# Second layer of a two-layer trunk: scores on 64 rows of the array, half of the projections and of the output projection placed between the attention steps

## The reference, cut to what matters

```python
def diff_attend(q, k, v, lam):
    s = jnp.einsum('bqhcd,bkhcd->bchqk', q, k).astype(jnp.float32) * HEAD_DIM ** -0.5
    p = jax.nn.softmax(s, axis=-1)
    a = (p[:, 0] - lam * p[:, 1]).astype(v.dtype)
    return jnp.einsum('bhqk,bkhv->bqhv', a, v)

# diff_attn_layer, the x branch (the layer's ctx output isn't needed)
q, k, v, g = jnp.split(h @ w_in, 4, axis=-1)      # k, v also of ctx
q = apply_rope(rms_norm(q, q_norm), cos, sin); k = apply_rope(rms_norm(k, k_norm), cos, sin)
o = diff_attend(q, k_all, v_all, lam)             # 512 queries, 768 keys
o = rms_norm(o, head_norm) * (1.0 - lambda_init)
x = x + gate * ((o * jax.nn.silu(g)) @ w_out)
```

## Time and profile before

| what | value |
|---|---|
| runs | 1311.74, 1316.6, 1316.97 us (median 1316.6) |
| the profiled execution, its own time | 1307.97 us |
| its span | 1306.1 us |
| busy in the span: PE, PE weight loads | 1234.6 us (95%), 673.1 us (52%) |
| DVE, ACT, POOL | 613.9 us (47%), 347.3 us (27%), 210.9 us (16%) |
| second layer's projections (window 791 to 1011) | PE busy 219.93 of 220 us |
| attention (window 1015 to 1247) | PE busy 219.50 of 232 us |
| output projection (window 1247 to 1302) | PE busy 54.97 of 55 us |

### The profile page before, as it was taken

The page is one execution under the profiler, slowest core; times in us unless marked ns, Lnnn a source line. Parts: engine busy times, 40 slices in busy tenths (PEclk is TensorE's granted clock), DMA queues, the critical chain, the costliest instruction groups (busy, mean ns, idle before and its releaser), DMA issues.

```text
span 1306.1 us, 12218 instructions
## 1 busy us (share of the span) xinstructions
PE 1234.6 (95%) x4455; PEld 673.1 (52%) x4455; DVE 613.9 (47%) x1224; ACT 347.3 (27%) x750; POOL 210.9 (16%) x198
## 2 busy tenths in 40 slices
PE   3699999999999999999899998999999999999988
PEld 0455566655555444555544444444444456667643
DVE  0466661368686645656711125330024444677712
ACT  1311112112221233335600012110011344566600
POOL 2100001567661300000000002230013000000000
PEclk9899999999999999999999999999999999999999
DMA  9601111034444011001000303110111110000001
GB/s 313 255 1 37 65 64 65 1 115 144 162 161 154 1 49 49 1 1 49 1 0 1 113 7 134 65 64 1 65 64 65 64 64 1 1 1 2 33 25 40
DMA packets 40464, 81.48 MB, mean 62 GB/s; under 512 B 2470, under 2 KB 3975, under 8 KB 40407
## 3 DMA queue, kind: packets, MB, share of 16 engines
q1 hardware_dynamic: 36165, 68.83, 15.0%
q10 hardware_dynamic: 3122, 8.57, 1.8%
q0 software_dynamic: 1120, 3.32, 0.9%
HBM read 78.58 MB, written 2.13 MB: 62 GB/s over the span
## 4 chain that ended last, share of the span: by engine, by line
PE 89%; DVE 5%; DMA 3%; ACT 2%; issue 1%; SPq 0%; POOLq 0%; POOL 0%; ACTq 0%; DVEq 0%
PE ps L623 42%; PE ps L859 9%; PE ps L800 6%; PE ps L886 6%; PE ps L906 3%; PE ps L753 3%; PE ps L842 3%; PE ps L782 3%; PE ps L769 2%; PE ps L897 2%; PE ps L662 2%; DMA ring<-in_mod_w_dram 1%; PE ps L823 1%; PE ps L833 1%; PE ps L816 1%
## 5 line engine op out<-in xcount | busy, mean ns | idle before, releaser
L623 PE MATMUL ps<-ring,hT 128*128 128x512 f32 (+1 forms) x960 | 397.2, 574 | 2.7 <-DVE hT L1016 1.3
L623 PEld LDWEIGHTS ps<-ring,hT 128*128 128x128 f32 x960 | 181.7, 190 | 208.7 <-issue 202.0
L623 PE MATMUL ps<-hT,ring 128*128 128x256 f32 (+1 forms) x512 | 169.2, 488 | 3.5 <-DVE pool_mem L1032 2.0
L1610 POOL TENSOR_SCALAR stat<-stat 128x8 f32<-128x8 f32 (+3 forms) x52 | 21.8, 419 | 768.7 <-DVE stat L1178 228.0
L623 PEld LDWEIGHTS ps<-hT,ring 128*128 128x128 f32 x512 | 96.1, 190 | 73.2 <-issue 65.8
L886 PE MATMUL ps<-pool_mem 128*128 128x512 f32 (+1 forms) x256 | 93.0, 487 | 1.3 <-ACT pool_mem L1547 1.3
L800 PE MATMUL ps<-ring,hT 128*128 128x512 f32 x192 | 89.3, 595 | 3.7 <-DVE pool_mem L1246 3.6
L1178 DVE TENSOR_REDUCE stat<-pool_mem 128x8 f32<-128x512 f32 (+1 forms) x26 | 18.6, 714 | 156.3 <-ACT pool_mem L1465 156.3
L859 PE MATMUL ps<-ring,hT 128*128 128x512 f32 x192 | 84.6, 593 | 1.6 <-DMA ring<-in_ev_w_out_dram 1.6
L1282 DVE TENSOR_TENSOR pool_mem<-ps,pool_mem 128x512 f32<-128x512 f32 x20 | 13.8, 691 | 138.0 <-PE ps L859 92.3
L1220 DVE TENSOR_REDUCE stat<-ps 128x1 f32<-128x768 f32 x64 | 61.1, 954 | 24.6 <-PE ps L886 24.4
(11 more groups left out here) (191 smaller groups left out, 1469.0 us busy)
## 6 DMA issues: line engine op xcount, KB each, us to landing
ring<-in_mod_w_dram SPq DMA_DIRECT2D x11, 2048.0 KB, 8.4
ring<-in_od_w_in_dram SPq DMA_DIRECT2D x8, 2048.0 KB, 7.9
ring<-in_ev_w_in_dram SPq DMA_DIRECT2D x7, 2048.0 KB, 7.9
ring<-in_ev_w_out_dram SPq DMA_DIRECT2D x4, 1536.0 KB, 6.7
ring<-in_od_w_out_dram SPq DMA_DIRECT2D x2, 2048.0 KB, 7.8
ring<-in_mod_w_dram ACTq DMA_DIRECT2D x1, 2048.0 KB, 15.6
xs_all<-in_x_dram POOLq DMA_DIRECT2D x4, 512.0 KB, 9.4
xs_all<-in_x_dram ACTq DMA_DIRECT2D x4, 512.0 KB, 5.4
```

The source lines that it names most:

```text
L623: mm = pe.matmul(bank[:, 0:width], lhs_of(k), rhs_of(k), start=(k == 0), stop=(k == count - 1))
```

## The change

The reference isn't changed, nor is the first layer. In the second:

- A score of one component uses only its 64 rows: queries are copied whole into `qT1` (one copy in place of two half copies, no zeroed halves), and the matmul takes rows 0 to 63 or 64 to 127 of both operands. All four score matmuls of a step stand together, alternating between components, and TensorE's stage for component 1 is empty. They wait for both exponentials of the step before.
- There is one probability buffer; transposes and value products belong to step n-1 in place of n-2, and the exponentials of step n wait for the transposes of step n-1. `comb1` is of step n itself.
- Before the attention stand only the first column halves of k1, q1, v1 (heads 0 to 3): 16 units. The rest, with g1, are 24 units between steps 0 and 19 (two in steps 1, 2, 3 and 9, one in the others). Their norm and rotary turn is a stage of its own, `rope`, which stands in the next step between `exp1` and `comb1`. The squares have two buffers.
- In a head's last step, the turns stand behind `exp1` in place of before it.
- `hnorm` and `otr` of a head are handed out in the same step, from step 12 on: heads 0, 1, 2 in steps 12, 13, 14, heads 3 to 6 in steps 16, 20, 24, 28, right behind the head's last `pv1`.
- The output projection is split over heads: `out1a` (heads 0 to 3, four matmuls a unit, 8 units: one in each of steps 21, 22, 24, 25, 27, 28 and two after the last step) and `out1` (heads 4 to 7, 8 units at the end). VectorE adds both to x.
- The gates' transfers and their sum come earlier (steps 11 and 16).

```diff
@@ stages_layer1
-    st += [("k1", n, t) for n in range(2) for t in range(NT)]
-    st += [("v1", n, t) for n in range(2) for t in range(NT)]
-    st += [("q1", n, t) for n in range(2) for t in range(NX)]
-    fill = [("g1", n, t) for n in range(2) for t in range(NX)]
+    for kind, tiles in (("k1", NT), ("q1", NX), ("v1", NT)):
+        for t in range(tiles):
+            st += [(kind, 0, t)] + ([("rope", kind, 0, t)] if kind != "v1" else [])
+
+    fill = [("g1", 0, 0)] + [u for t in range(1, 4) for u in (("g1", 0, t), ("k1", 1, t - 1))]
+    fill += [("k1", 1, t) for t in range(3, NT)]
+    fill += [("q1", 1, t) for t in range(NX)] + [("v1", 1, t) for t in range(NT)]
+    gate_fill = [("g1", 1, t) for t in range(NX)]
+    early_out = [("out1a", n, t) for n in range(2) for t in range(NX)]
...
-    for n in range(len(work) + 2):
+    for n in range(len(work) + 1):
         if n < len(work):
-            st.append(("sc1",) + work[n] + (0,))
-        if n >= 2:
-            st.append(("ptr1",) + work[n - 2])
+            st += [("sc1",) + work[n] + (c,) for c in range(2)]
+        if n >= 1:
+            st.append(("ptr1",) + work[n - 1])
         if n < len(work):
             h, t = work[n]
-            st.append(("sc1", h, t, 1))
+            st.append(("exp1", h, t))
             if t == NX - 1 and h < C_HEADS - 1:
                 st += [("hk", h + 1, 1), ("hq", h + 1), ("hk", h + 1, 0)]
-            st.append(("exp1", h, t))
...
+            st += ropes
+            ropes = []
+            st.append(("comb1", h, t))
+        now = []
+        if n < 16:
+            now = [fill.pop(0) for _ in range(1 + (n in (1, 2, 3, 9)))]
+        elif n < 20:
+            now = [gate_fill.pop(0)]
+        elif early_out and n % 3 != 2:
+            now = [early_out.pop(0)] if len(early_out) > 2 else []
+        st += now
+        ropes += [("rope",) + u for u in now if u[0] in ("k1", "q1")]
+        if n >= 1:
+            st.append(("pv1",) + work[n - 1])
+            if work[n - 1][1] == NX - 1:
+                late += [("hnorm", work[n - 1][0]), ("otr", work[n - 1][0])]
...
+        if n >= 12 and n < len(work):
+            for _ in range(2):
+                if late:
+                    st.append(late.pop(0))
+    st += late[:1] + early_out + late[1:]
     st += [("out1", n, t) for n in range(2) for t in range(NX)]
@@ tensor engine
                 elif kind == "sc1":
...
+                    if c == 1:
+                        continue
                     if n == 0:
                         pe.wait_ge(prob_ready, len(SCORE))
-                    if n >= 2:
-                        pe.wait_ge(prob1_ready, n - 1)
+                    else:
+                        pe.wait_ge(prob1_ready, n)
...
                     for lo, hi in ((0, 512), (512, TOK)):
-                        mm = pe.matmul(pair(n)[:, lo:hi], qpad[:, c, t * P:(t + 1) * P], kT1[:, lo:hi],
-                                       start=True, stop=True)
-                    mm.then_inc(sc_ready, 1)
+                        for comp in range(2):
+                            half = slice(comp * HD, (comp + 1) * HD)
+                            mm = pe.matmul(pair(n + comp)[:, lo:hi], qT1[half, t * P:(t + 1) * P], kT1[half, lo:hi],
+                                           start=True, stop=True)
+                            if hi == TOK:
+                                mm.then_inc(sc_ready, 1)
...
+                    (w,) = slabs(stage)
+                    project(stage, SLAB, lambda k: oT[first + k][:, a[1] * P:(a[1] + 1) * P],
+                            lambda k: w[:, first + k, :], C_HEADS // 2)
@@ scalar engine
-                        A.copy(qpad[0:HD, 0, :], bank[0:HD, :])
-                        A.copy(qpad[HD:P, 1, :], bank[HD:P, :]).then_inc(done_sem(stage), 1)
+                        A.copy(qT1, bank).then_inc(done_sem(stage), 1)
...
-                        if n < 4:
-                            act.wait_ge(qk_ready, len(HEADU))
-                        else:
-                            act.wait_ge(pt1_ready, n // 2 - 1)
-                        A.activation(place[:, c, :], pair(n)[:, 0:TOK], ACT.Exp, bias=nmax[:, r:r + 1],
+                        if n >= 2:
+                            act.wait_ge(pt1_ready, n // 2)
+                        A.activation(prob1[:, c, :], pair(n)[:, 0:TOK], ACT.Exp, bias=nmax[:, r:r + 1],
                                      scale=SCALE, accum_out=rsum[:, r:r + 1]).then_inc(prob1_ready, 1)
```

More of the change, by code:

```diff
@@ L177, in stages_layer1 @@
-        if 1 <= n <= len(work):
-            st.append(("comb1",) + work[n - 1])
-        if fill and (n < 4 or n % 2 == 0):
-            st.append(fill.pop(0))
-        if n >= 2:
-            st.append(("pv1",) + work[n - 2])
-            if late and not fill:
-                st.append(late.pop(0))
-            if work[n - 2][1] == NX - 1:
-                late += [("hnorm", work[n - 2][0]), ("otr", work[n - 2][0])]
-            if work[n - 2] == (C_HEADS - 1, 1):
-                st.append(("gates", 1))
@@ L189, in stages_layer1 @@
-    st += late + [("gatesum", 1)]
+                if h + 1 == 3:
+                    st.append(("gates", 1))
+            st += ropes
[10 more added lines that the diff above has]
+        ropes += [("rope",) + u for u in now if u[0] in ("k1", "q1")]
@@ L215 @@
 UNIT_STAGES = ("params", "mod", "modsum", "modcol", "xbc", "kvdt", "dt", "q", "ga", "z", "pv", "ytr", "out0",
-               "k1", "v1", "q1", "g1", "hq", "hk", "pv1", "otr", "out1")
+               "k1", "v1", "q1", "g1", "hq", "hk", "pv1", "otr", "out1a", "out1")
 UNITS = [s for s in STAGES if s[0] in UNIT_STAGES]
@@ L235, in slabs_of @@
         return [(kind, stage[1])]
+    if kind == "out1a":
+        return [("out1", stage[1])]
     return []
@@ L868, in _ @@
                     pe.wait_ge(qk_ready, NT + HEADN[("q1", h // 4, NX - 1)] + 1)
-                    turn(stage, [q1v[:, t, h * P:(h + 1) * P] for t in range(NX)])
+                    turn(stage, [q1v[:, h // 4, t, h % 4 * P:(h % 4 + 1) * P] for t in range(NX)])
                 elif kind == "hk":
                     h, s = a
-                    pe.wait_ge(qk_ready, NT + HEADN[("k1", 1, NT - 1)] + 1)
-                    turn(stage, [k1v[:, t, h * P:(h + 1) * P] for t in (range(NX) if s == 0 else range(NX, NT))])
+                    pe.wait_ge(qk_ready, NT + HEADN[("k1", h // 4, NT - 1)] + 1)
+                    turn(stage, [k1v[:, h // 4, t, h % 4 * P:(h % 4 + 1) * P]
+                                 for t in (range(NX) if s == 0 else range(NX, NT))])
                 elif kind == "sc1":
@@ L901, in _ @@
                     pe.wait_ge(pt1_done, at(*stage))
-                    if stage == ("pv1", 0, 0):
-                        wait_done_upto(pe, ("v1", 1, NT - 1))
+                    if t == 0 and h % 4 == 0:
+                        for tile in range(NT):
+                            wait_done(pe, ("v1", h // 4, tile))
                     bank = begin(stage)
@@ L911, in _ @@
                     turn(stage, [g1v[:, t, a[0] * P:(a[0] + 1) * P] for t in range(NX)])
-                elif kind == "out1":
+                elif kind in ("out1a", "out1"):
+                    first = 0 if kind == "out1a" else C_HEADS // 2
                     if a == (0, 0):
-                        wait_done_upto(pe, ("otr", C_HEADS - 1))
-                    token_major(stage, a[1])
+                        for h in range(first, first + C_HEADS // 2):
+                            wait_done(pe, ("otr", h))
+                    (w,) = slabs(stage)
+                    project(stage, SLAB, lambda k: oT[first + k][:, a[1] * P:(a[1] + 1) * P],
+                            lambda k: w[:, first + k, :], C_HEADS // 2)
         @block.vector
@@ L1279, in _ @@
                         tmp, gate = res_tmp1[:, u % 2, :], gate_bc1[:, n * SLAB:(n + 1) * SLAB]
+                    if stage == ("out1", 0, 0):
+                        dve.wait_ge(early_ready, 2 * NX)
                     if u >= 2:
-                        dve.wait_ge(x1_ready if kind == "out0" else out_ready, u - 1)
+                        dve.wait_ge(told, u - 1)
                     V.tensor_tensor(tmp, bank_of(stage), gate, ALU.mult).then_inc(done_sem(stage), 1)
@@ L1284, in _ @@
                     part = x1[:, t, n * SLAB:(n + 1) * SLAB]
-                    V.tensor_tensor(part, part, tmp, ALU.add).then_inc(x1_ready if kind == "out0" else out_ready, 1)
+                    V.tensor_tensor(part, part, tmp, ALU.add).then_inc(told, 1)
                 elif kind == "g1":
@@ L1305, in _ @@
                                                 in1=rsum[:, r:r + 1], op0=ALU.mult, op1=ALU.mult))
[L1306 removed]
+                    p0, p1 = (prob1[:, c, :] for c in range(2))
                     V.scalar_tensor_tensor(out=p0, in0=p1, scalar=rinv[:, r + 1:r + 2], in1=p0,
@@ L1555, in _ @@
                     h, t = a
-                    place = prob1[at(*stage) % 2]
```

(2 more changed lines are left out.)

59 lines of the change are left out of this document (31 added, 28 removed).

## The result

| | kernel before | changed kernel |
|---|---|---|
| median (lowest to highest) | 1313.03 us (1307.8 to 1316.97), 10 runs | 1321.05 us (1316.58 to 1326.4), 10 runs |
| ratio | | 1.006, interval 1.0038 to 1.0082 |
| profiled execution: time, span, granted clock | 1307.97, 1306.1, 0.996 | 1319.4, 1316.8, 0.984 |

The change made the kernel slower by 0.6%. I had forecast 5 us less; it is 8 us more. The time lies inside the range, but the sign is wrong.

A forecast was written before the change was run, and what follows sets the result against it. TensorE was taken to bound the second layer; 456 us of work plus 50 of waits gave 506 in place of 511.1, moving the median 5 us to 1311.5. The 8-in-10 range was 1296 to 1327.

The forecast's parts named there:

- the sign: Whole kernel: median to move 5 us down to 1311.5; chances faster 0.36, within 0.5% 0.40, slower 0.24.
- Scores: Second layer's attention: both components run side by side, 1.29 us a step, 41.3 us less work.
- rivals of partial and no pairing: Each step's four score matmuls: partial overlap gives 1325 (chance 0.08), no overlap +41, 1353 (chance 0.07).
- the 1.72 us: Scores of a step if passes start strictly in turn: 1.72 in place of 1.29, 13.8 more in all.
- Change of the array's shape: Going in and out of 64-row scores costs 0.20 us a step, 6.4 in all; bounds 0 and 0.3.
- Waits: TensorE's waits in the second layer, listed by place: 50 us after the change, 20 before.
- step 10's: Two rotary turns after step 9's two q units end comb1 at 13.4; 1.75 us of wait come through.
- late first passes: After each of some 25 waits the first pass runs late by about 0.08 us: 2 us.
- granted clock 1.00 throughout: Listed among the signs that would show the forecast right: the granted clock stays at 1.00.
- the clock as a rival: Steps from 20 on: clock drop over half of 95 us costs about 25 us, giving 1336; chance 0.04.
- the 506 forecast: Second layer, start to start: 456 us of work plus 50 of waits, in place of 511.1.
- longer waits: Rival: each of the eleven long waits is longer by 1 us, giving 1322; chance 0.05.

The follow-up runs named there:

- e6: Changed kernel with both components' scores computed on rows 0 to 63, so nothing can run side by side: 1376.31 us, ratio 1.048 to the kernel before.
- e4: Changed kernel with matmuls whose result nobody reads inside TensorE's waits before third turns and otr: 1308.64 us, ratio 0.9964 to the kernel before.
- e9: Kernel before, unedited, profiled a second time: 1314.24 us, ratio 1.0008.
- e1: Changed kernel with only the turns put back in front of the exponentials: 1303.12 us, ratio 0.9926 to the kernel before.
- e2: Changed kernel with only otr moved one step behind its hnorm: 1299.13 us, ratio 0.9895 to the kernel before.
- e3: Changed kernel with turns back in front of the exponentials and otr one step behind its hnorm: 1284.22 us, ratio 0.9778 to the kernel before.
- e5: Kernel before with only the 64-row scores of both components together, nothing else of the change: 1305.94 us, ratio 0.9941.
- e7: Changed kernel with turns before exponentials, otr a step behind hnorm, and unread matmuls meant for the remaining waits: 1282.15 us, ratio 0.9765 to the kernel before.
- e8: Kernel before with unread matmuls meant for its two long waits, at the layer boundary and the last otr: 1312.45 us, ratio 1.0001.

## Why the prediction was wrong, point by point

- **Scores.** Right. Both components together take half, shown by e6 (1.28 us a step, 1.29 forecast). The rivals of partial and no pairing are refuted. In the trace of the changed kernel the components' passes start 6 to 7 ns apart, though the queue gives one component's two passes before the other's. The queue's order can be read from e6, where the second and the fourth of a step's four 256-column passes raise the semaphore of the scores (992.350 and 992.782); in the changed kernel the two that raise it start together (970.979 and 970.985), after both components' first passes (970.763 and 970.770). Where the Trainium skill's "TensorE: Matmul & The Clock Gate", Part 3, has strict program order, this measurement decides against the 1.72 us that I worked out from it.
- **Change of the array's shape.** Nearly right: 1.49 from the first score to the transposes. What I missed lies outside: transposes and products take until the next scores 0.15 us more than their work (10.51 against 10.35 for a step). Over some 27 steps that TensorE paces this is 4 us.
- **Waits.** Right as a list. Turns 7 x 2.53 (2.6 forecast); step 10's 1.35 (1.75, though its own 13.4 less 11.8 gives 1.6); `otr` in steps 24 and 28 2.81 (2.8), in 16 3.87 (2.8: GpSimd's root takes 2.02 us there and 1.01 in steps 24 and 28; VectorE adds up the gates beside it from 1134.75 on, but no run shows that as the cause); steps 12 to 14 1.70 (1.8); step 20 with the one before 4.5 (4.1); empty steps 5.03 to 5.11 (5.05 to 5.2); the end 3.0 (2.6); `otr` to `out1` 1.25 (1.05). They add up to 48.6 us, for 48 forecast. (Each is the idle time in the trace plus the 0.16 us by which records overlap in a stream. The forecast's 2 us for late first passes are not among them; no run measured those by themselves.)
- **The clock.** This is the step that failed: "granted clock 1.00 throughout", and the clock as a rival at 0.04. From 791.3 (where its projections would have begun at full clock) to 1312.9 the layer takes 521.6 us, 15.6 more than the 506 forecast. Of these the passes in the seven low stretches lost 12.5, and the steps' 0.15 us make the rest of it but for a microsecond. e4 shows the clock as the cause: from its first unit (792.74) to its last pass, without a low stretch, it takes 509.6 us, 3.6 over the forecast. My rival had the right mechanism but the wrong form: I looked for it in the steps from 20 on, as one long drop for low busy shares. It came as separate short stretches, each behind a single wait, in the busiest part too.
- **What misled me** was the earlier trace rows with the earlier trace rows: a window of 60 us at 1.00 that contains a wait of 2.8 us. From this one execution I concluded that such waits are free. e9 shows the same kernel paying at the same wait in another execution. The Trainium skill's "TensorE: Matmul & The Clock Gate", Part 1, describes a matmul loop that falls to half clock again at each of its waits of 3 to 5 us. The rows of the changed kernel agree in part: it does so at 7 of its 16 waits, which are of 1.7 to 3.9 us.
- **The base.** The profiled execution of before was one of its best, with 0.996 where the median is 0.991. Clock lost, as (1 - clock) x span, is 11.8 us in the median for before and 22.4 for the changed kernel. So some 9 to 11 us of the difference are clock (9 if each us of this measure is counted as the 0.85 us of span that goes with it among the runs of before). The remaining spans, clock x span, are 1299.5 and 1297.6: 2 us less, where I forecast 5 less and 4 of work came back. 11 - 2 = 9, against the 8 us between the medians. That the range held the result is luck in this sense: it was drawn for failing pairs and longer waits, not for the clock, whose price I had at 25 us and 0.04.

**Where the gain went.** The cheaper scores take 30 us out of TensorE's work (41 less 11 for the changes of shape). What two parts of the plan cost was measured one edit at a time: turns behind the exponentials 17 us (e1), `otr` in the step of its `hnorm` 22 us (e2), together 37 us (e3), of which 29 are waits (12.4 and 16.9) and the rest clock. The remainder of the plan (units spread over the steps, split output projection, one buffer) was worth having: e5, without it, is 8 us under before by its ratio, and e3, with it, 29. Its parts were not measured one by one.

## What to carry to other kernels

Price each new wait of 2 to 4 us on TensorE at its own length and, in 7 cases of 16 here, 1.8 us more on average for the matmuls behind it at half clock; with sixteen such waits that is 12 us, more than many a change gains. One profile at full clock doesn't show that its waits are free: compare the granted clock of several executions before taking one as the base. When a stage leaves a wait at a head's end, look first at what stands in front of the releasing instruction in its engine's queue; here two moves in the list gave 2.8%. When you fill a wait with unread matmuls, look in the trace whether they run in it: an engine can wait for more than one semaphore, and matmuls placed behind the one that comes last are added work (e7 and e8, 1.9 us each).

## What was not expected of the hardware

- A drop of the clock can follow waits as short as 0.9 us where several stand close together (e8: 0.94 and 0.89 us, then 0.50 from 1243.5 on), and need not follow one of 2.65 us (first profile of the kernel before).
- The low stretches of the attention keep their places between the two profiled executions of the changed kernel (six of six; the one at the boundary is in one of them only), and change them when an edit elsewhere shifts the program (e2).
- Score passes of 64 rows give the two halves of the array work at once, 6 to 7 ns apart, and cost 0.15 us a step around them, beside the 0.20 that they take from first score to transposes.
- What is open: which wait drops the clock. Length alone doesn't tell (waits of 2.53 us that end at 954.07 and 1062.19 of the changed kernel cost nothing more, the same at 1006.70 cost 1.7), and no run here varied one wait by itself.
